# An encoder layer on one core: when sums between stages are taken, when banks are emptied, and how a second half's first pass walks its tiles

## What is computed

```python
r = x + 0.5 * post_ffn1(SwiGLU_1(pre_ffn1(r)))      # FFN: 1024 -> 2 x 2816 -> 1024
u = pre_mix(r);  z = u @ w_in                       # q, k, v, b, c, xv
r = r + post_mix(concat(norm_A(attention), norm_B(b * conv3(c * xv))) @ w_out)
r = r + 0.5 * post_ffn2(SwiGLU_2(pre_ffn2(r)))
r = r + post_ple(sigmoid(pre_ple(r) @ w_ple_gate) * (p @ w_ple_proj))

def rms_norm(x, g):
    return x * rsqrt(mean(x * x, -1) + 1e-6) * g
```

## Time and profile before

| | us |
|---|---|
| median of 3 runs | 1111.8 (1111.7 to 1114.43) |
| the profiled execution | 1111.88 |
| its span, first to last instruction | 1110.1 |
| TensorE matmuls busy (share) | 1061.6 (96%) |
| VectorE busy | 700.3 (63%) |
| ScalarE busy | 510.2 (46%) |
| GpSimd busy | 287.5 (26%) |
| mean granted TensorE clock | 0.983 of full |

### The profile page before, as it was taken

The page is one execution under the profiler, slowest core; times in us unless marked ns, Lnnn a source line. Parts: engine busy times, 40 slices in busy tenths (PEclk is TensorE's granted clock), DMA queues, the critical chain, the costliest instruction groups (busy, mean ns, idle before and its releaser), DMA issues.

```text
span 1110.1 us, 20077 instructions
## 1 busy us (share of the span) xinstructions
PE 1061.6 (96%) x8095; PEld 1029.5 (93%) x8095; DVE 700.3 (63%) x1057; ACT 510.2 (46%) x927; POOL 287.5 (26%) x222
## 2 busy tenths in 40 slices
PE   5999999999999999999999889899999999999896
PEld 5999999999999999777889889899999999998896
DVE  6998777777311297656592789877777651127743
ACT  4545555556322253423434553555555551226563
POOL 4114344340211141000313421343443121113321
PEclk8999999999999999999999999999999999999998
DMA  7314334335322232111232212243342532333002
GB/s 220 90 43 115 98 94 115 83 97 155 110 76 71 57 82 76 48 35 49 56 88 77 77 51 64 77 115 91 100 115 77 156 92 69 103 95 92 24 1 81
DMA packets 182679, 94.76 MB, mean 85 GB/s; under 512 B 11769, under 2 KB 180929, under 8 KB 182593
## 3 DMA queue, kind: packets, MB, share of 16 engines
q1 hardware_dynamic: 182576, 93.56, 30.6%
q10 hardware_dynamic: 16, 0.00, 0.0%
HBM read 91.15 MB, written 2.50 MB: 84 GB/s over the span
## 4 chain that ended last, share of the span: by engine, by line
PE 80%; DVE 13%; ACT 2%; issue 2%; POOL 1%; DMA 1%; DVEq 0%; SPq 0%; ACTq 0%; POOLq 0%
PE bank L1630 13%; PE bank L1632 13%; PE bank L1631 12%; PE bank L1730 9%; PE bank L1733 9%; PE bank L1732 9%; PE bank L1660 4%; PE misc L1782 2%; PE misc L1845 2%; PE misc L1730 2%; PE misc L1733 2%; PE misc L1732 2%; PE misc L1824 1%; DVE w_split L1063 1%; DVE r L1084 1%
## 5 line engine op out<-in xcount | busy, mean ns | idle before, releaser
L1632 PE MATMUL bank<-h_hi,w_split 128*128 128x272 f32 x704 | 204.5, 290 | 0.0
L1630 PE MATMUL bank<-h_hi,w_split 128*128 128x272 f32 x704 | 204.3, 290 | 0.0
L1631 PE MATMUL bank<-h_lo,w_split 128*128 128x272 f32 x704 | 202.8, 288 | 0.0
L1063 DVE TENSOR_TENSOR w_split<-raw,w_split 128x1408 fp32r<-128x1408 f32 (+2 forms) x66 | 98.8, 1510 | 156.0 <-ACT w_split L631 156.0
L563 POOL TENSOR_TENSOR ssq<-ssq,sq 128x272 f32<-128x272 f32 x112 | 107.7, 961 | 239.7 <-ACT sq L636 229.4
L1631 PEld LDWEIGHTS bank<-h_lo,w_split 128*128 128x128 f32 x704 | 133.2, 189 | 0.2
L1630 PEld LDWEIGHTS bank<-h_hi,w_split 128*128 128x128 f32 x704 | 133.0, 189 | 0.3
L1632 PEld LDWEIGHTS bank<-h_hi,w_split 128*128 128x128 f32 x704 | 132.9, 189 | 0.0
L1730 PE MATMUL bank<-t_hi,even_blocks 128*128 128x272 f32 x432 | 126.3, 292 | 6.5 <-issue 3.7
L1733 PE MATMUL bank<-t_hi,even_blocks 128*128 128x272 f32 x432 | 125.6, 291 | 0.0
L1732 PE MATMUL bank<-t_lo,even_blocks 128*128 128x272 f32 x432 | 125.0, 289 | 0.0
(11 more groups left out here) (243 smaller groups left out, 2656.2 us busy)
## 6 DMA issues: line engine op xcount, KB each, us to landing
raw_up<-w_ffn_gate_up SPq DMA_DIRECT2D x88, 512.0 KB, 4.9
raw<-w_ffn_down SPq DMA_DIRECT2D x32, 704.0 KB, 4.7
raw<-w_in SPq DMA_DIRECT2D x14, 512.0 KB, 4.3
raw<-w_ple_gate SPq DMA_DIRECT2D x8, 512.0 KB, 3.8
x_tok<-x_prompt SPq DMA_DIRECT2D x4, 512.0 KB, 4.8
raw<-w_in SPq DMA_DIRECT2D x8, 256.0 KB, 3.8
raw<-w_out SPq DMA_DIRECT2D x16, 128.0 KB, 3.4
raw<-w_out SPq DMA_DIRECT2D x8, 256.0 KB, 3.6
```

The costliest lines, as they stand in the source:

```text
L1063: nc.vector.tensor_tensor(chunk_part(c, 1), chunk_raw(c), chunk_part(c, 0).bitcast(F32), ALU.subtract).then_inc(lo_made, 1)
L1630: nc.tensor.matmul(psum(u), wh, hi, start=(k == 0), stop=False)
L1631: nc.tensor.matmul(psum(u), wh, lo, start=False, stop=False)
L1632: mm = nc.tensor.matmul(psum(u), wl, hi, start=False, stop=(k == n - 1))
```

## The change

At down1 to mix and at down2 to ple, the sum of r's half A is no longer taken in down's last group but in the next stage's first pass: at mix at k = 5, together with y's half B sum; at ple at k = 2, with y's half B sum at k = 6. At down1 to mix and out to up2 the sums n0 + 1 and n0 + 2 change roles: n0 + 1 is now y's half B and n0 + 2 r's half A (`SUM_HALF`, `SUMMED`), so that chain B's inversion comes first. The inversion into `rpre` for half A moves from `last_group` into chain B, after its tile 1 (mix, up2), or directly ahead of chain B (ple). The evacuations of half A's first banks go into chain B earlier: mix after tiles 2 and 3, and units 2 and 3 after tile 5; up2 `up_scale(s, 0)` after 2 and `up_scale(s, 1)` after 4; ple `ple_gate(0)` ahead of the chain. ScalarE's first Silu gates of up2 go behind its chain, its first sigmoids of ple ahead of its chain. The first pass of half B in mix and up2 does k = 0 to 2 (`LEAD` = 3) for units 0 and 1, then for 2 and 3, then k = 3 to 7 for all four units a tile. Its sum (r's half B) is taken behind the second unit's low pass.

```diff
--- before.py
+++ after.py
@@ -70,6 +70,8 @@
     NCHUNK = chunks
     DOWN_GROUPS = KD // 2
 
+    LEAD = 3
+
     slot_of = [(c + (2 if c >= C0["mix"] + MIX.index("b2") else 0)) % SLOTS for c in range(NCHUNK)]
 
     before = [max([b for b in range(c) if slot_of[b] == slot_of[c]], default=None) for c in range(NCHUNK)]
@@ -132,7 +134,10 @@
     SUM0 = {"start": 0, "down1": 2, "mix": 6, "out": 10, "down2": 14, "ple": 18}
 
 
-    SUMMED = [8, 16, 30, 38, 40, 48, 52, 62, 60, 64, 76, 87, 88, 96, 110, 118, 120, 128, 140, 144]
+
+
+    SUM_HALF = [A, B] + [A, B, A, B] + [A, A, B, B] + [A, B, A, B] + [A, A, B, B] + [A, B]
+    SUMMED = [8, 16, 30, 40, 38, 48, 52, 62, 60, 64, 76, 88, 87, 96, 110, 118, 120, 128, 140, 144]
 
     PLE_UNITS = [(i, h) for g in (0, 2) for h in (A, B) for i in (g, g + 1)]
 
@@ -422,13 +427,9 @@
 
         TOKEN_SUMS = [((0, 1), misc[:, 3]), ((2, 3, 4), bank[:, 3])]
 
-        def sum_half(n):
-
-            return n if n < 2 else n % 2 if n >= SUM0["ple"] else (n - 2) // 2 % 2
-
         def sum_place(n):
 
-            return 2 * (n % 2) if SUM0["mix"] <= n < SUM0["out"] else sum_half(n)
+            return 2 * (n % 2) if SUM0["mix"] <= n < SUM0["out"] else SUM_HALF[n]
 
         def sum_bank(n):
 
@@ -796,17 +797,16 @@
                 split_hi(c + SLOTS + 2)
                 if with_p:
                     p_hi(2)
-                root(n0 + 1, D)
                 step(B, 1)
                 split_hi(c + SLOTS + 3)
+                root(n0 + 1, D)
                 root(n0 + 2, D)
 
             def up_stage(n, s, d, ci, s_b, n_pre):
 
                 c0 = C0[s]
-                chain(ci, B, s_b, {4: lambda: up_gate(s, 0)} if ci else {2: lambda: root(0, D)})
-                if not ci:
-                    up_gate(s, 0)
+                chain(ci, B, s_b, {} if ci else {2: lambda: root(0, D)})
+                up_gate(s, 0)
                 up_gate(s, 1)
                 root(n_pre, D)
                 split_hi(c0 + 4), split_hi(c0 + 5)
@@ -1033,7 +1033,8 @@
                                              ACT.Sqrt, bias=eps[0:DEC], scale=1.0 / D)
                 i.then_inc(tok_rooted, 1)
 
-            chain(3, B, SQ0["ple"] - KD, {3: lambda: ple_gate(0)})
+            ple_gate(0)
+            chain(3, B, SQ0["ple"] - KD)
             ple_square(0)
             ple_gate(1)
             ple_square(1)
@@ -1244,8 +1245,8 @@
 
                 c0 = C0[s]
                 if ci:
-                    chain_r(ci, B, y, n_pre - 1, {4: lambda: up_scale(s, 0)})
-                    up_scale(s, 1)
+                    chain_r(ci, B, y, n_pre - 2, {1: lambda: invert(n_pre - 1, rpre[:, A, :]),
+                                                  2: lambda: up_scale(s, 0), 4: lambda: up_scale(s, 1)})
                     up_hidden(s, 0), up_hidden(s, 1)
                     chain_lo(ci, B)
                 else:
@@ -1304,18 +1305,18 @@
                 chain_r(ci, A, y, n0, {3: splits} if ci == 2 else {KD - 1: splits})
                 if with_p:
                     p_lo(0), p_lo(1)
+                    chain_lo(ci, A, range(0, KD // 2))
                 split_lo(c + SLOTS + 2)
                 if with_p:
                     p_lo(2)
-                if ci != 2:
-                    invert(n0 + 1, rpre[:, A, :])
+                    chain_lo(ci, A, range(KD // 2, KD))
+                elif ci != 2:
                     chain_lo(ci, A, range(0, KD // 2))
                 split_lo(c + SLOTS + 3)
-                if ci != 2:
+                if ci == 2:
+                    chain_lo(ci, A)
+                elif not with_p:
                     chain_lo(ci, A, range(KD // 2, KD))
-                else:
-                    chain_lo(ci, A)
-                    invert(n0 + 1, rpre[:, A, :])
 
             def down_stage(s, ci):
                 g0, last, n = C0[s], DOWN_GROUPS - 1, FFN[s]
@@ -1514,10 +1515,13 @@
                 dve.wait_ge(sinks_made, 7)
 
             c0 = C0["mix"]
-            chain_r(1, B, y_down, SUM0["down1"] + 2, {4: lambda: (evacuate(0), evacuate(1))})
-            for v in range(2, len(MIX_UNITS)):
+            chain_r(1, B, y_down, SUM0["down1"] + 1, {1: lambda: invert(SUM0["down1"] + 2, rpre[:, A, :]),
+                                                      2: lambda: evacuate(0), 3: lambda: evacuate(1),
+                                                      5: lambda: (evacuate(2), evacuate(3))})
+            for v in range(3, len(MIX_UNITS)):
                 d = v - MIX_ATTN0
-                evacuate(v)
+                if v > 3:
+                    evacuate(v)
                 if v == 3:
                     chain_lo(1, B)
                     invert(SUM0["down1"] + 3, rpre[:, B, :])
@@ -1597,7 +1601,9 @@
                     nc.vector.scalar_tensor_tensor(out, out_banks(tt)[0:n, part, :], rstd_tok[0:n, tt:tt + 1], out,
                                                    ALU.mult, ALU.add).then_inc(out_made, 1)
 
-            chain_r(3, B, y_down, SUM0["down2"] + 2, {3: lambda: ple_gate(0)})
+            invert(SUM0["down2"] + 1, rpre[:, A, :])
+            ple_gate(0)
+            chain_r(3, B, y_down, SUM0["down2"] + 2)
             ple_mul(0)
             ple_gate(1)
             chain_lo(3, B)
@@ -1643,13 +1649,13 @@
                 k = n - SUM0["mix"]
                 if k == 1:
                     pe.wait_ge(exp_made, NTASK)
-                src = ssm[:, k, :] if 0 <= k < 4 else ssq[:, sum_half(n), :]
+                src = ssm[:, k, :] if 0 <= k < 4 else ssq[:, SUM_HALF[n], :]
                 nc.tensor.matmul(sum_bank(n), ones[:], src, start=True, stop=True).then_inc(sum_done, 1)
 
-            def hi_pass(pair, high, h, wait, hooks={}):
-
-
-                for k in range(KD):
+            def hi_pass(pair, high, h, wait, hooks={}, ks=range(KD)):
+
+
+                for k in ks:
                     wait(k)
                     if k in hooks:
                         hooks[k]()
@@ -1669,13 +1675,17 @@
                                           start=False, stop=(k == KD - 1))
                 mm.then_inc(unit_done, 1)
 
-            def first_units(units, ci, h, hooks_hi={}, hooks_lo={}, second={}):
+            def first_units(units, ci, h, hooks_hi={}, hooks_lo={}, second={}, lead=KD):
+
 
                 def high(k, h):
                     return x_high(ci, k, h)
-                hi_pass(units[0:2], high, h, lambda k: pe.wait_ge(x_hi_made, 16 * ci + 8 * h + k + 1), hooks_hi)
-                if units[2:4]:
-                    hi_pass(units[2:4], high, h, lambda k: None, second)
+
+                def arrived(k):
+                    pe.wait_ge(x_hi_made, 16 * ci + 8 * h + k + 1)
+                hi_pass(units[0:2], high, h, arrived, hooks_hi, range(0, lead))
+                hi_pass(units[2:4], high, h, lambda k: None, second, range(0, lead))
+                hi_pass(units, high, h, arrived, {**hooks_hi, **second}, range(lead, KD))
                 for n, (u, c, _) in enumerate(units):
                     lo_pass(u, c, lambda k, h: x_low(ci, k, h), h,
                             None if n else lambda k: pe.wait_ge(x_ready, 16 * ci + 8 * h + k + 1))
@@ -1740,8 +1750,10 @@
                     if h == A:
                         first_units(units, ci, A, hooks_hi, {}, second)
                     else:
-                        sums = {4 if ci else 2: lambda: all_sums(n_pre)}
-                        first_units(units, ci, B, {} if ci else sums, {0: after_b}, sums if ci else {})
+                        if ci:
+                            first_units(units, ci, B, {}, {1: lambda: all_sums(n_pre)}, {}, LEAD)
+                        else:
+                            first_units(units, ci, B, {2: lambda: all_sums(n_pre)}, {0: after_b})
                 for p in range(4, 2 * NCL):
                     for m in range(2):
                         up_ready(s, p, m)
@@ -1804,7 +1816,7 @@
 
             up_stage(0, "up1", 0, {}, {2: lambda: all_sums(0)}, 1, turn_gains)
             n0 = SUM0["down1"]
-            down_stage("down1", 0, {0: {5: lambda: all_sums(n0)}, 1: {17: lambda: all_sums(n0 + 1)}})
+            down_stage("down1", 0, {0: {5: lambda: all_sums(n0)}})
 
 
             def scores(d, g):
@@ -1878,9 +1890,9 @@
             for h in (A, B):
                 units = [(U0["mix"] + v, C0["mix"] + v % 4, lambda v=v: mix_ready(v)) for v in range(4 * h, 4 * h + 4)]
                 if h == A:
-                    first_units(units, 1, A, {4: lambda: all_sums(n0 + 2)})
+                    first_units(units, 1, A, {5: lambda: (all_sums(n0 + 1), all_sums(n0 + 2))})
                 else:
-                    first_units(units, 1, B, {}, {}, {4: lambda: all_sums(n0 + 3)})
+                    first_units(units, 1, B, {}, {1: lambda: all_sums(n0 + 3)}, {}, LEAD)
             for v, (tile, h) in list(enumerate(MIX_UNITS))[8:]:
                 mix_ready(v)
                 product(U0["mix"] + v, x_tiles(1, C0["mix"] + MIX.index(tile), h))
@@ -1949,7 +1961,7 @@
 
```

(5 more changed lines are left out.)

## The result

The changed kernel takes 1116.78 us (median of 6 runs, 1115.74 to 1118.03), the kernel before 1112.36 us beside it (6 runs): a ratio of 1.0039, 95% interval 1.0027 to 1.0051, so 4.3 us slower (3.0 to 5.7). The forecast was 1117.

A forecast was written before the change was run, and what follows sets the result against it. TensorE, 96% busy, was taken as the main bound, with VectorE equally late at M; M +4.8, U +2.4 and P -2.2 gave +5.0 us on 1111.8, say 1117. Forecast 1115 to 1119 (0.50); range 1110.5 to 1120.5.

The forecast's parts named there:

- M: Boundary down1 to mix: the late last sum leaves VectorE idle 3.7 us and delays the ninth unit; +4.8 us.
- rival 1: Bank waits stay short and VectorE meets the last sum in time: M +1.3, P -2.4, about 1112; chance 0.25.
- the clock: At M, the 3.6 us stop brings a half-clock stretch: +1.4 us, some 0.3 hidden in a later wait.
- U: Boundary out to up2: gates behind ScalarE's chain delay low parts, last sum and the first Strassen product; +2.4 us.
- the table load: At U, between chain end and first gate: 1.28 us counted; the skill's drain, 1.4 us worse, left out.
- P: Boundary down2 to ple: the 3.34 us first-gate wait goes, a 2.1 us wait before r's transposes comes; -2.2 us taken.
- the -1.5 that I had named for that case: At P: the gain is -1.5 us instead of -2.4 if the 2.1 us stop costs the clock.
- Rival 2: TensorE is the only bound and the change does what its layout is for: -8, or 1104; chance 0.10.
- Rival 3: Clock cascade: each new stop costs a half-clock stretch; M 6.5, U 3.5, P -1.5: +8.5, or 1120; chance 0.15.
- rival 4: SP's loads and POOL's adds: POOL's fortieth sum is done just ahead of its new place; 0.5 us if not.

The follow-up runs named there:

- the run with the gate in the chain: The changed kernel with the first Silu gate of up2 put back after tile 4 of ScalarE's chain: 1116.75 us, 1.0039 to the kernel before.
- the early sums: The changed kernel with the last sums at down1 to mix and out to up2 taken at k = 7 of the shared pass: 1110.64 us, 0.9976.
- the sink rows: Routing sinks moved to the last step (v == 8), in the changed kernel: 1114.87 us, 1.0022; in the kernel before: 1111.64 us, 0.9992.
- U alone: The kernel before with only the out to up2 part of the change: 1113.07 us, 0.9997.
- P alone: The kernel before with only the down2 to ple part of the change: 1110.51 us, 0.9974.
- M's alone: The changed kernel with only the last sum at down1 to mix moved to k = 7 of the shared pass: 1113.09 us, 1.0006.
- the best version above: The changed kernel with both last sums at k = 7, six low parts ahead of up2's hidden products, sink rows at the last step: 1108.83 us, 0.9969.

## Why the forecast held, step by step

**M, forecast +4.8, found +5.4.** All times of after here less 1.75. Half A's start: 400.3 (forecast 400.4). Last sum: 425.6 (425.8). The pass began 0.4 us later than I had it (413.7), and its 80 matmuls up to the sum took 11.9 us instead of 12.45: 1.9 us more than 80 x 0.125, where I had 2.45. (The two bracketed waits, 0.53 and 0.59, count less than the pace shows, because a matmul's busy time overlaps the next one's.) So rival 1 was right about part of the bank waits, and two errors of about 0.5 us cancelled in the place of the sum. End of VectorE's low parts: 423.1 (423.3). Idle ahead of the inversion: 3.62 (3.7). Ninth unit: 431.7 (431.9). What was undersized is the clock: I had 1.1 net for one stretch, and the trace shows 1.9, from the ninth unit (+3.5) to the first transpose (+5.4), with the whole of 431.90:438.70 at 0.50 (1.2 GHz). In the trace of the run with the gate in the chain, whose code at M is the same, only 3.4 us are at 0.50 and M costs +4.5, so that the forecast lies between two executions. The step that TensorE's own savings buy nothing because VectorE is last is what the early sums and the sink rows showed.

**U, forecast +2.4, found +1.8 at the first Strassen product, and +0.4 behind it.** Less 7.04, the shift at up2's start: third bank's wait 0.92 (forecast 1.05), low parts begin 651.7 (652.05), sum 656.4 (657.0), inversion 657.6 (658.1), split 659.5 (660.0). The steps are 0.3 to 0.6 us early, because the chain ends 0.5 earlier than I summed (648.05 for 648.6), and the order of the waits is as forecast. The step that failed came behind these: I let a delay of the first Strassen product pass through to the end. It did not: here the granted clock behind it is full, where it was half before. Before and after, in the windows that follow that product, the granted clock is the last figure but two:

```profile
701.40:704.80 3.40, 3.40 (x16) 3.40 (x16) 2.69 (x4) 2.62 (x4) 0.00 (x0) 0.51 0.93 251
```

```profile
710.20:713.60 3.40, 3.40 (x27) 3.40 (x28) 2.69 (x4) 2.51 (x4) 0.00 (x0) 1.00 0.93 253
```

16 matmuls against 27, 11 x 0.125 = 1.4 us, the price I had from the earlier trace rows. The wait ahead of it is 2.81 us instead of 3.48, but its length alone does not decide: with U alone it is 3.50 and the clock stays full as well:

```profile
704.44:707.84 3.40, 3.40 (x27) 3.40 (x28) 2.69 (x4) 2.60 (x4) 0.00 (x0) 1.00 0.98 269
```

Further up in U, the stretch behind the wait of 2.31 us is gone, as forecast. One that I had not forecast came at 670.80:674.20, behind TensorE's wait of 3.28 us at 669.36 for VectorE to read a bank; VectorE is late there, so that the first Strassen product moved no more than VectorE's split did (+1.8 both):

```profile
670.80:674.20 3.40, 3.40 (x17) 3.40 (x16) 3.25 (x5) 1.21 (x2) 0.00 (x0) 0.50 0.82 224
```

On the table load: the first gate starts 0.01 us after its end (656.31 and 1.28, then 657.60), although the load is on VectorE's path now. The Trainium skill (ScalarE: Activation LUTs, What ACT_TABLE_LOAD costs) gives 1.28 us of load and 1.38 of drain. The 1.28 agrees, and no row here shows the drain; leaving it out was right.

**P, forecast -2.2, found -1.5.** Less 7.40, the shift at down2's start: first gate read 1029.4 (forecast 1029.6), inversion 1030.6 (1030.8), transposes 1040.0 (1040.0), the wait ahead of them 2.22 (2.1), and no half-clock stretch. Up to there it was -3.3, as forecast. The 2.2 us stop did not cost the clock, and so the -1.5 is not the -1.5 that I had named for that case; it is the same figure reached another way. Then I had the root of the last sum and its inversion follow 2.2 us earlier; the inversion came 1.3 us earlier (1057.96 less 7.40, against 1051.90). The term that was mis-sized is VectorE's low parts: six take 3.75 us, in the kernel before 2.56:

```profile
1043.84 2.56 DVE L1093 SCALAR_TENSOR_TENSOR x_lo<-r,gT,x_hi_a 128x272 fp32r<-128x272 f32 x6
```

What differs beside them is GpSimd. It adds up squares for 2.32 of the 3.75 us in the changed kernel, and is idle in the kernel before (0.02 us busy over 1043.84:1046.31):

```profile
1048.04 1.79 POOL L564 TENSOR_TENSOR ssq<-ssq,sq 128x272 f32<-128x272 f32 x2
1049.78 0.62 POOL L561 COPY ssq<-sq 128x272 f32<-128x272 f32 x1
1050.54 0.78 POOL L564 TENSOR_TENSOR ssq<-ssq,sq 128x272 f32<-128x272 f32 x1
```

The y products behind the low parts, ScalarE's squares of them, its output copy and the root are one chain. The low parts begin 2.5 us earlier and end 1.3 us earlier, and so does what follows. That GpSimd is the cause is read from the rows; no run took its additions away. P alone, by its median, gained 2.9 us and not 1.5 (above), so that the size of P's step is less sure than the one trace makes it look.

**The rivals.** Rival 1 (no stall at the last sum) was wrong because of the place of the sum: it is about what happens when the sum is moved forward (1113.09 with M's alone). Rival 2's time (1104) no kernel reached. Rival 3 (a stretch behind each stop) was right only behind M's long wait: the granted clock is 1.00 through M's shared pass, through U's slow low pass and behind P's stop. Of rival 4, GpSimd's fortieth addition ended at 404.61, and both sums follow at 404.71, at most 0.2 us late. The terms were off by +0.6 (M), -2.0 (U) and +0.7 (P) and partly cancel, so that the total (5.0 for 4.3) is nearer than U's term: in that the forecast was lucky. That 1117 hits the median of 1116.78 so closely is luck as well, because the kernel before took 0.5 us more beside it than the 1111.8 that I started from.

## What to carry to other kernels

When work is put closer together on the busiest engine, ask first where the small reductions stand in its queue: a sum of 0.5 us moved 32 matmuls back stopped VectorE for 3.6 us and with it the split that the busiest engine needed. At M two engines finished together, and there a gain on one bought nothing and a delay on the other was paid whole. Put a reduction right where its input is complete (at M that was 4.4 us before the sum was taken), and fill a wait for another engine with work that doesn't depend on it.

## What the runs showed of the hardware

**The same wait may or may not be followed by half clock.** Behind waits of 2.1 to 3.5 us the granted clock was at either level: 0.51 behind the 3.48 us ahead of the first Strassen product of the kernel before, 1.00 behind 3.50 us at the same place with U alone; 0.50 behind the 2.12 us at M with the sink rows moved, full behind the 2.22 us at P in the changed kernel. In down2 every trace has the same wait of 2.25 or 2.26 us for the low parts of p; the clock behind it is 0.50 in the kernel before and in the changed kernel, and 1.00 in the best version above. So the length of the wait alone does not decide, and what does is not shown by these runs. A stretch of 3.4 us at half clock costs 1.4 us when TensorE is otherwise busy, a third of what this change moved, and two single traces can differ by one such step or more for that reason alone.

**VectorE is slower beside GpSimd when it reads two tensors from SBUF.** The changed kernel's trace has 64 low parts, which read two tensors from SBUF. The 43 that run beside no GpSimd instruction take 0.49 to 0.50 us; the 21 that overlap one take 0.85 on average and 1.03 at most. The scalings of y by a sum (`misc` is in PSUM), which read one tensor from PSUM and one from SBUF, take 0.42 to 0.44 us beside GpSimd and without it. In the best version above six low parts at U take 4.11 us with GpSimd busy for 2.29 of them, where eight take 3.38 in the changed kernel with GpSimd idle. The Trainium skill (SBUF — State Buffer, SBUF: two separate sides) says that the two share a pair of ports, that whoever starts first holds it for the whole instruction, and that a VectorE operation with two SBUF inputs contends for it. The durations agree with that, though no row here shows a lock itself. A schedule that moves VectorE's work earlier has to count what GpSimd does there.

**The start of an execution varies.** The first matmul of up1 came between 16.84 and 19.25 us in the traces here, in kernels whose code up to there is the same. Any comparison of two single executions has to take that off first.
